# A two-layer encoder trunk: four slots for the one-hot rows of the expert spread, and gather slots that turn over four, then six

## What is computed

```python
def block(args):                      # 128 tokens at a time, 2 blocks
    x_blk, i_blk, g_blk = args        # rows, 128 expert numbers, 128 gates a token
    act = jax.nn.gelu(jnp.einsum('td,ted->te', x_blk, u[i_blk], preferred_element_type=jnp.float32))
    return jnp.einsum('te,ted->td', (g_blk * act).astype(v.dtype), v[i_blk])
```

## Time and profile before

| | us |
|---|---|
| median of 3 runs (lowest, highest) | 3355.64 (3353.34, 3356.28) |
| the profiled execution, its own time | 3357.06 |
| its span in the trace | 3355.3 |
| TensorE matmul busy | 2093.6 (62%) |
| VectorE busy | 2600.2 (77%) |
| ScalarE busy | 1269.1 (38%) |
| GpSimd busy | 1606.6 (48%) |

### The profile page before, as it was taken

One profiled execution on the slowest core, in us unless ns is written; L12 is line 12 of the kernel. 1 busy time (PEld: TensorE's weight loads), 2 busy tenths in 40 slices (PEclk: granted clock), 3 DMA queues, 4 the chain that ended last, 5 costly groups with the idle time before them and its releaser, 6 DMA issues.

```text
span 3355.3 us, 25410 instructions
## 1 busy us (share of the span) xinstructions
PE 2093.6 (62%) x7428; PEld 1389.1 (41%) x7428; DVE 2600.2 (77%) x3749; ACT 1269.1 (38%) x3645; POOL 1606.6 (48%) x1051
## 2 busy tenths in 40 slices
PE   7999964421330069999929998444032104999994
PEld 6887853320220054444418787333022104444441
DVE  4454589999999976655685758999999998666667
ACT  4444344445875570000003543444477647100000
POOL 1000065666666626654560004666665762566655
PEclk9999987765555579999969999666555556999997
DMA  6554689999989939999984448999998994899999
GB/s 231 180 186 138 228 356 419 419 386 388 346 310 355 402 106 402 409 407 408 408 312 152 137 138 344 420 417 391 385 347 313 363 382 169 323 409 409 409 408 357
DMA packets 247609, 1096.43 MB, mean 327 GB/s; under 512 B 23208, under 2 KB 23984, under 8 KB 176944
## 3 DMA queue, kind: packets, MB, share of 16 engines
q0 software_dynamic: 147456, 805.37, 60.7%
q1 hardware_dynamic: 96640, 282.22, 22.6%
q10 hardware_dynamic: 3376, 7.23, 0.6%
HBM read 1092.63 MB, written 2.11 MB: 326 GB/s over the span
## 4 chain that ended last, share of the span: by engine, by line
DVE 37%; DMA 27%; PE 19%; issue 8%; POOL 7%; ACT 2%; ACTq 0%; SPq 0%; DVEq 0%; POOLq 0%
DVE ring_sb L1888 23%; DMA actT_sb<-in_peer_vg_dram,idx_all 16%; PE bank L1041 15%; DMA ring_sb<-in_peer_vg_dram,idx_all 5%; DMA ring_sb<-in_peer_u_dram,idx_all 4%; DVE x_sb L1879 3%; POOL ring_sb L600 3%; POOL actT_sb L615 3%; DVE gain L1861 2%; PE bank L1306 1%; POOL ring_sb L615 1%; ACT gain L838 1%; DVE shared L1617 1%; DVE shared L1613 1%; DVE pair_all L1621 1%
## 5 line engine op out<-in xcount | busy, mean ns | idle before, releaser
L600 POOL DMA_INDIRECT ring_sb<-in_peer_u_dram,idx_all x496 | 917.2, 1849 | 504.1 <-DVE idx_all L1622 362.1
L1879 DVE SCALAR_TENSOR_TENSOR x_sb<-actT_sb,gate_rows,x_sb 128x1024 f32<-128x1024 f32 x340 | 434.6, 1284 | 234.2 <-DMA actT_sb<-in_peer_vg_dram,idx_all 227.7
L1888 DVE CUSTOM_DVE_ANT_0 ring_sb<-ring_sb,arena 128x2048 f32<-128x2048 f32 x256 | 572.9, 2287 | 23.9 <-DMA ring_sb<-in_peer_u_dram,idx_all 23.3
L615 POOL DMA_INDIRECT actT_sb<-in_peer_vg_dram,idx_all x340 | 421.9, 1241 | 352.6 <-DVE x_sb L1879 300.0
L1888 DVE CUSTOM_DVE_ANT_0 ring_sb<-ring_sb,actT_sb 128x2048 f32<-128x2048 f32 x256 | 573.0, 2287 | 0.0
L1041 PE MATMUL bank<-w_parts,actT_hi 128*128 128x512 f32 x1664 | 521.7, 395 | 7.1 <-DVE w_parts L416 5.0
L1319 PE MATMUL bank<-ring_sb,arena 128*128 128x512 f32 x1024 | 485.3, 596 | 6.4 <-DMA ring_sb<-in_peer_vd_dram 4.1
L1319 PE MATMUL bank<-ring_sb 128*128 128x512 f32 x1024 | 482.5, 594 | 0.0
L1306 PE MATMUL bank<-gain 128*128 128x128 f32 x1024 | 223.6, 392 | 341.1 <-DVE gain L1861 159.4
L416 DVE TENSOR_TENSOR w_parts<-ring_sb,w_parts 128x2048 fp32r<-128x2048 f32 x100 | 229.7, 2302 | 212.9 <-ACT w_parts L410 212.7
L1088 PE MATMUL bank<-arena 128*128 128x256 f32 x896 | 249.6, 445 | 209.4 <-DVE shared L1888 209.2
(11 more groups left out here) (199 smaller groups left out, 2431.6 us busy)
## 6 DMA issues: line engine op xcount, KB each, us to landing
ring_sb<-in_peer_vd_dram SPq DMA_DIRECT2D x128, 1024.0 KB
ring_sb<-in_mlstm_w_in_dram SPq DMA_DIRECT2D x48, 1024.0 KB, 5.1
arena<-in_peer_wq_dram SPq DMA_DIRECT2D x28, 1024.0 KB, 13.7
ring_sb<-in_attn_w_in_dram SPq DMA_DIRECT2D x20, 1024.0 KB, 5.1
ring_sb<-in_mlstm_w_out_dram SPq DMA_DIRECT2D x16, 1024.0 KB, 5.0
ring_sb<-in_attn_w_out_dram SPq DMA_DIRECT2D x16, 1024.0 KB, 5.0
ring_sb<-in_peer_u_dram,idx_all POOLq DMA_INDIRECT x496, 10.7
actT_sb<-in_peer_vg_dram,idx_all POOLq DMA_INDIRECT x340
```

The lines of the kernel that those rows point to most:

```text
L600: nc.gpsimd.indirect_dma_start(out=ring[i % NU], out_offset=None, in_=u_tab[l], in_offset=bass.IndirectOffsetOnAxis(ap=rows_at, axis=0),). ...
L615: nc.gpsimd.indirect_dma_start(out=g_slot[j % NG], out_offset=None, in_=vg_tab[l], in_offset=bass.IndirectOffsetOnAxis(ap=idx_all[b][:, p: ...
L1879: v.scalar_tensor_tensor(out=xb[b][:, DENSE:D], in0=g_slot[j % NG], scalar=w_all[b][:, p:p + 1], in1=xb[b][:, DENSE:D], op0=ALU.mult, op1= ...
L1888: v.tensor_tensor_reduce(ring[i % NU], ring[i % NU], rows[b], 1.0, 0.0, ALU.mult, ALU.add, dots[u % 2][:, k:k + 1]).then_inc(dot_done, 1)
```

## The change

Eight tiles are spread over `gain` and over `rows_1`; block 0 goes on using two slots of each kind, and block 1 takes four, so the writer of a tile of group g waits for group g-4. ScalarE makes two one-hot tiles ahead instead of one. Since `rows_1` is taken during the spread of block 1, the value gathers turn over four slots for j = 0 to 11, and over all six from j = 12 on; gather 16, the first into `rows_1`, waits until all matmuls of the spread are done. Gather j waits for the add of the gather that had its slot last.

```diff
-        onehot_2 = [gain[:, i * CH:(i + 1) * CH].rearrange("p (t e) -> p t e", e=P) for i in range(2)]
-        weighted_1 = [gain[:, (2 + i) * CH:(3 + i) * CH].rearrange("p (t e) -> p t e", e=P) for i in range(2)]
+        spread = [gain[:, i * CH:(i + 1) * CH].rearrange("p (t e) -> p t e", e=P) for i in range(4)]
+        spread += [rows_1[:, i * CH:(i + 1) * CH].rearrange("p (t e) -> p t e", e=P) for i in range(4)]
+        onehot_2, weighted_1 = spread[0::2], spread[1::2]
+        DEPTH = [2, 4]
+        def wait_spread(eng, l, b, g):
+            if g >= DEPTH[b]:
+                eng.wait_ge(wb_full, (2 * l + b) * GROUPS + g - DEPTH[b] + 1)
+            elif b or l:
+                eng.wait_ge(wb_full, (2 * l + b) * GROUPS)
...
+        G_EARLY = 12
+        G_SLOT = [j % 4 if j < G_EARLY else (j - G_EARLY) % NG for j in range(NB * PICKS)]
+        G_USE = [G_SLOT[:j].count(G_SLOT[j]) for j in range(NB * PICKS)]
+        G_BEFORE = [max([-1] + [i for i in range(j) if G_SLOT[i] == G_SLOT[j]]) for j in range(NB * PICKS)]
```

GpSimd, in `values(l, j)`:

```diff
-                elif j < NG:
-                    pool.wait_ge(dot_done, (l + 1) * LAYER_TILES)
-                else:
-                    pool.wait_ge(vg_added, l * NB * PICKS + j - NG + 1)
+                if j == G_EARLY + 4:
+                    pool.wait_ge(wb_full, (2 * l + 2) * GROUPS)
+                if G_BEFORE[j] >= 0:
+                    pool.wait_ge(vg_added, l * NB * PICKS + G_BEFORE[j] + 1)
```

ScalarE, in `onehot_group(b, g)` and in the order of the second block:

```diff
-                    done = (2 * l + b) * GROUPS + g
-                    if done >= 2:
-                        act.wait_ge(wb_full, done - 1)
-                    if g == 0 or b:
+                    wait_spread(act, l, b, g)
+                    if g < 2:
...
                 onehot_group(1, 1)
+                onehot_group(1, 3)
                 for g in range(GROUPS):
                     weights_group(1, g)
-                    if g % 2 and g + 2 < GROUPS:
-                        onehot_group(1, g + 2)
+                    if g % 2 and g + 4 < GROUPS:
+                        onehot_group(1, g + 4)
```

VectorE, in `weighted_group(b, g)`:

```diff
-                    at = (2 * l + b) * GROUPS + g
-                    if at >= 2:
-                        dve.wait_ge(wb_full, at - 1)
+                    wait_spread(dve, l, b, g)
```

More of the change, by code:

```diff
@@ L315, in trunk_kernel, with value_landed @@
         G_ORDER = [(j % NB, j // NB) for j in range(NB * PICKS)]
+        G_EARLY = 12
+        G_SLOT = [j % 4 if j < G_EARLY else (j - G_EARLY) % NG for j in range(NB * PICKS)]
+        G_USE = [G_SLOT[:j].count(G_SLOT[j]) for j in range(NB * PICKS)]
+        G_BEFORE = [max([-1] + [i for i in range(j) if G_SLOT[i] == G_SLOT[j]]) for j in range(NB * PICKS)]
+        def value_landed(l, j):
+            return 16 * (l * G_SLOT.count(G_SLOT[j]) + G_USE[j] + 1)
         D_PAIRS = P // 2
@@ L610, in values @@
                     pool.wait_ge(dot_done, l * LAYER_TILES + LAYER_TILES - NU + 8)
-                elif j < NG:
-                    pool.wait_ge(dot_done, (l + 1) * LAYER_TILES)
-                else:
-                    pool.wait_ge(vg_added, l * NB * PICKS + j - NG + 1)
+                if j == G_EARLY + 4:
+                    pool.wait_ge(wb_full, (2 * l + 2) * GROUPS)
+                if G_BEFORE[j] >= 0:
+                    pool.wait_ge(vg_added, l * NB * PICKS + G_BEFORE[j] + 1)
                 nc.gpsimd.indirect_dma_start(
-                    out=g_slot[j % NG], out_offset=None, in_=vg_tab[l],
+                    out=g_slot[G_SLOT[j]], out_offset=None, in_=vg_tab[l],
                     in_offset=bass.IndirectOffsetOnAxis(ap=idx_all[b][:, p:p + 1], axis=0),
-                ).then_inc(vg_landed[j % NG], 16)
+                ).then_inc(vg_landed[G_SLOT[j]], 16)
             def experts(l):
@@ L828, in onehot_group @@
                 def onehot_group(b, g):
-                    done = (2 * l + b) * GROUPS + g
-                    if done >= 2:
-                        act.wait_ge(wb_full, done - 1)
-                    if g == 0 or b:
+                    wait_spread(act, l, b, g)
+                    if g < 2:
                         at = GR[f"t{l}"] + b
                         act.wait_ge(tr_out[at % 2], at // 2 + 1)
+                    rows = onehot_2[g % DEPTH[b]]
                     for j in range(GROUP):
                         t = GROUP * g + j
-                        st.did(nc.scalar.activation(onehot_2[g % 2][:, j, :], numbers, ACT.Abs,
+                        st.did(nc.scalar.activation(rows[:, j, :], numbers, ACT.Abs,
                                                     bias=picks_T[:, P + t:P + t + 1], scale=-1.0))
                     st.need(st.n)
-                    nc.scalar.activation(onehot_2[g % 2], onehot_2[g % 2], ACT.Relu, bias=1.0,
+                    nc.scalar.activation(rows, rows, ACT.Relu, bias=1.0,
                                          scale=-1.0).then_inc(onehot_act, 1)
@@ L1305, in weights_group @@
                     for j in range(GROUP):
-                        last = mm(mis[g % 2][:, j * P:(j + 1) * P], onehot_2[g % 2][:, j, :], weighted_1[g % 2][:, j, :],
+                        last = mm(mis[g % 2][:, j * P:(j + 1) * P], onehot_2[g % DEPTH[b]][:, j, :],
+                                  weighted_1[g % DEPTH[b]][:, j, :],
                                   start=True, stop=True, skip_group_check=True)
@@ L1854, in weighted_group @@
                 def weighted_group(b, g):
-                    at = (2 * l + b) * GROUPS + g
-                    if at >= 2:
-                        dve.wait_ge(wb_full, at - 1)
+                    wait_spread(dve, l, b, g)
                     for j in range(GROUP):
                         t = GROUP * g + j
-                        last = v.tensor_scalar(weighted_1[g % 2][:, j, :], numbers, picks_T[:, t:t + 1],
+                        last = v.tensor_scalar(weighted_1[g % DEPTH[b]][:, j, :], numbers, picks_T[:, t:t + 1],
                                                picks_T[:, 2 * P + t:2 * P + t + 1], ALU.is_equal, ALU.mult)
@@ L1864, in weighted_group @@
                     if b == 1 and g % 2 == 0:
-                        v.tensor_tensor(onehot_2[0], numbers.unsqueeze(1).to_broadcast([P, GROUP, P]),
+                        v.tensor_tensor(onehot_2[g % DEPTH[b]], numbers.unsqueeze(1).to_broadcast([P, GROUP, P]),
                                         picks_T[:, P + GROUP * g:P + GROUP * (g + 1)].unsqueeze(2).to_broadcast([P, GROUP, P]),
@@ L1873, in add_value @@
                     b, p = G_ORDER[j]
-                    dve.wait_ge(vg_landed[j % NG], 16 * uses(j, l, NG, NB * PICKS))
+                    dve.wait_ge(vg_landed[G_SLOT[j]], value_landed(l, j))
                     if l * NB * PICKS + j >= NB:
@@ L1878, in add_value @@
                         dve.wait_ge(weight_done, (l + 1) * LAYER_TILES)
-                    v.scalar_tensor_tensor(out=xb[b][:, DENSE:D], in0=g_slot[j % NG], scalar=w_all[b][:, p:p + 1],
+                    v.scalar_tensor_tensor(out=xb[b][:, DENSE:D], in0=g_slot[G_SLOT[j]], scalar=w_all[b][:, p:p + 1],
                                            in1=xb[b][:, DENSE:D], op0=ALU.mult, op1=ALU.add).then_inc(vg_added, 1)
```

## The result

| | before | changed |
|---|---|---|
| median of 4 runs, us (lowest to highest) | 3355.19 (3353.34 to 3356.28) | 3330.58 (3327.35 to 3333.53) |
| ratio, 95% interval | | 0.9927 (0.9910 to 0.9944) |
| the profiled execution, us (span) | 3357.06 (3355.3) | 3329.58 (3327.7) |

The account below looks back on a forecast made before the run. The serial spread was taken to bound the kernel: 8.0 + 8.9 = 16.9 us saved in two layers, less 0.4 for gathers, is 16.5; from 3357.06 that gives 3340.6, stated as 3340 us, range 3332 to 3350.

Parts of the forecast that it names:

- What bounds it: Spread of the second block: a serial stage, 63.8 and 64.7 us; shortening it by X moves all that follows by X.
- ScalarE sets the pair: Spread: with tiles made ahead, a fast pair of groups is ScalarE's, 3.58 us instead of 4.02; a slow one TensorE's, 4.18.
- The start doesn't move: Start of the spread: copies of groups 0 and 1 still wait for the first matmuls, so nothing is gained there.
- the share of slow time: Spread: a third of the time at TensorE's lower clock, against today's 41%; 55.8 us a layer, 16.9 us saved together.
- Rival 1: Spread: TensorE's clock stays up throughout, saving 23.7 us, 3333 us in total; chance 0.17.
- Dense part: Values part after the spread: TensorE and the DMA engines are full, so it keeps its length and only begins earlier.
- Fewer value slots: Gathers at the spread's end: later issue and VectorE's earlier finish cancel, two fewer gathers landed; 0.2 us lost a layer.
- The hole before gather 15: GpSimd's queue after the spread: gather 15 waits for gather 11's slot, landed at 7.8 and added at 9.1 us.
- rival 4: GpSimd's queue at gather 15: gather 11 lands after 10 us, not 3.3; 9.3 us lost a layer, 3370 us; chance 0.04.
- The range: Whole kernel: 3332 to 3350 us, from the forecast's own bounds of 3334 to 3350 and two more at the lower end.

Follow-up runs that it names:

- e9: Kernel before, with four extra 128x128 products on TensorE before each odd group of the second block from group 5 on: 3347.67 us against 3352.95, ratio 0.9984.
- e10: Changed kernel with one more ScalarE copy in each pair, and extra TensorE products from group 6 on: 3340.01 us against 3352.95 for the kernel before, ratio 0.9965.
- e6: Changed kernel with one more 128x384 copy on ScalarE in each pair of groups: 3344.91 us against 3353.56 for the kernel before, ratio 0.9976.
- e1: Kernel before with only the new value slots; two slots per tile kind and ScalarE's old order: 3356.41 us against 3352.62, ratio 1.0010.
- e7: Changed kernel with all its slots but ScalarE's old order: 3349.03 us against 3353.56 for the kernel before, ratio 0.9986.
- e3: Changed kernel's order with four one-hot and three weighted tiles placed so that all six value slots stay in use: 3328.71 us, ratio 0.9929 to the kernel before.
- e5: Changed kernel, but gathers 12 and 13 take the two empty value slots and 14 to 17 the used ones: 3327.21 us, ratio 0.9925 to the kernel before.

## Why the prediction was wrong, point by point

- *What bounds it*: right. The spread is serial, and what it lost the whole gained: 24.5 of the 27.5 us between the two profiled executions.
- *ScalarE sets the pair*: right, 3.53 us instead of 3.58. Two copies back to back are 0.81 us apart, below the 0.86 that I had called the lower bound (a bound from a copy and another kind of instruction), and from the copy to L854 it is 0.89 instead of 0.86; the rest came as expected. Fourteen pairs 0.05 shorter are 0.7 us a layer; the last two copies are 2.4 us apart, not 2.3.
- *The start doesn't move*: right (copy 0 came 6.9 us after the last dot before and after).
- **The step that failed is the share of slow time**, "I take a third". It was none: pairs of 3.53 in both layers of the changed kernel, granted clock 1.00. Copy 1 to copy 31 came to 51.9 and 51.8 us where I had 55.8: 7.9 us in both layers, of which the shorter pairs are 1.1 and the clock is 6.8. 16.5 + 7.9 = 24.4 is close to the 24.5 between the medians, in part by luck: the two profiled executions are 27.5 us apart, of which 2.0 lie behind the spread and 1.0 elsewhere. Rival 1, at 0.17, was the case. I had listed TensorE's idle third against it; its idle time is 1.5 of 3.53 us, more than a third, and the clock stayed up all the same. My own reason for less slow time, 2.34 of 3.58 us busy against 2.34 of 4.02, does not hold either: in one piece the products of a pair take 2.02 us, so the busy share did not rise. e9 and e10 show that the clock in this kernel depends on what TensorE is given to do in its idle time, and a shorter pair brings its products closer together by itself; whether their number or the shorter gap counts is open. The rule of the Trainium skill ("TensorE: Matmul & The Clock Gate", A second HAM failure mode: psum-queue depth-cycling), which I set against the change, would have the clock swing on, as the two banks are still cycled with 1.5 us idle in each pair. The trace of the changed kernel does not agree (1.00), while e6, with the same banks and pairs of 4.10 us, does (0.83).
- *Dense part*: I said that it keeps its length. It lost 4.1 us in both layers together, since it no longer begins slow, and the part after it took back 2.1.
- *Fewer value slots*: two effects that cancel; confirmed by the parts, e1 (+3.4 us by its ratio) and e7 against e1 (-8). Taken by themselves they are larger than I had worked out, and part of the run-ahead's gain is used up in the changed kernel: e7 leaves 34 and 28 adds for after the dense part, the changed kernel 37 and 31. I put that down to the shorter spread, which has less idle DMA time in it; no run shows this alone. e3 shows the sum: no loss that can be measured.
- *The hole before gather 15*: it was there as described, but longer. Gather 11 was added 7.1 us after it was out, not 3.3, with gathers 12 to 14 in flight beside it. That is rival 4's mechanism with 3.8 us more in place of 7; e5, without the hole, is at most some 2 us faster.
- *The range* missed by 1.4 us: it left out the upper clock together with what that brings the dense part (2.0 us net in the profiled executions).

## What to carry to other kernels

When a chain that goes round between two engines is broken by deeper buffers, look at the order in which the fuller engine does its work too: e7 has all the buffers and none of the speed in the spread. The buffers are what allows the new order, and bring little there by themselves. Where TensorE's clock swings between its levels in a stage that is to become denser, work out the sum for the upper level as a case of full weight, not as a rival. And buffers taken from a transfer cost little where the engines of that transfer are idle, if the engine that frees the others is made to run ahead.

## What was unexpected of the hardware

- The same 4.10 us pairs ran with a granted clock of 0.83 and 0.84 (e6) and of 0.98 to 1.00 (e10), with nothing changed but four products, 1.06 us in all, in TensorE's idle time of a pair.
- At the upper clock TensorE was busy for about the same share of a pair before (53 to 59%) and in the changed kernel (57%), and the granted clock was 0.81 and 0.78 in the one and 1.00 in the other.
- Filling TensorE with useless work made the kernel before faster: in e9 all pairs but one are 4.02 us, and the ratio is 0.9984 (0.9975 to 0.9993).
- An indirect DMA on GpSimd that takes 0.94 us took 4.13 us in the changed kernel while VectorE added without a pause (6.52 before). Both times it was done 0.8 us after the last of these adds, so the next gather left only when the burst was over.
